# A two-block transformer kernel: table loads by another queue, weight splitting moved around evictions, and the compression's weave re-dealt

## What is computed

```python
h = rms_norm(x, norm_mix)
cols = split_columns(h @ w_in)
o_a = nsa_mixer(cols, ...)      # compressed, selected and window attention
o_b = swa_mixer(cols, ...)      # window attention with sinks
o_c = fox_mixer(cols, ...)      # causal attention with forget gates
proj = jnp.einsum('btnm,nmd->btnd', stack([o_a, o_b, o_c]), w_branch)
gates = jax.nn.sigmoid(cols['merge']).reshape(b, t, 3, 1024)
x = x + (gates * proj).sum(axis=2) @ w_out
x = x + conv_ffn(rms_norm(x, norm_ffn), w_gate, w_up, conv_w, conv_b, w_down)
```

## Time and profile before

| what | value |
|---|---|
| times of the runs | 1562.22, 1564.59, 1554.29 us; median 1562.22 |
| the profiled execution | 1554.0 us |
| its span | 1552.2 us |
| its mean granted TensorE clock | 0.988 |
| PE busy | 1460.3 us, 94% |
| PEld busy | 1196.3 us, 77% |
| DVE busy | 993.6 us, 64% |
| ACT busy | 754.2 us, 49% |
| POOL busy | 67.6 us, 4% |
| DMA | 202.84 MB, mean 131 GB/s |

### The profile page before, as it was taken

How to read it: one execution, slowest core, us unless ns; L and a number is a source line. 1 busy time by engine, 2 the same in 40 slices (tenths; PEclk the granted TensorE clock), 3 DMA queues, 4 the chain that set the end, 5 groups by cost and what they waited for, 6 DMA issues and landing times.

```text
span 1552.2 us, 24143 instructions
## 1 busy us (share of the span) xinstructions
PE 1460.3 (94%) x9392; PEld 1196.3 (77%) x9392; DVE 993.6 (64%) x2286; ACT 754.2 (49%) x1630; POOL 67.6 (4%) x76
## 2 busy tenths in 40 slices
PE   6999999999999999999988999997999899999999
PEld 4777766777778777888766777676787798799987
DVE  3647677564667548545585668766777576777763
ACT  4436566453655443241224546655566347555542
POOL 0000000110000000020000100001101020000000
PEclk9999999999999999999999999999999999999999
DMA  9131180222470322221371144434435542445554
GB/s 364 57 109 55 52 319 25 102 82 68 163 258 1 103 94 82 95 82 55 130 264 54 55 151 110 164 87 139 159 127 157 200 163 93 156 155 187 187 188 136
DMA packets 59866, 202.84 MB, mean 131 GB/s; under 512 B 7694, under 2 KB 10984, under 8 KB 59624
## 3 DMA queue, kind: packets, MB, share of 16 engines
q1 hardware_dynamic: 53568, 192.84, 35.8%
q10 hardware_dynamic: 6008, 7.40, 2.1%
q0 software_dynamic: 176, 1.06, 0.2%
HBM read 199.43 MB, written 1.84 MB: 130 GB/s over the span
## 4 chain that ended last, share of the span: by engine, by line
PE 70%; DVE 15%; DMA 5%; ACT 4%; issue 3%; POOL 2%; SPq 0%; ACTq 0%; DVEq 0%; POOLq 0%
PE ps L2253 65%; PE ps L2256 5%; DVE w_l L2923 3%; DMA w_raw<-in_l_out 1%; DVE st L3022 1%; ACT w_h L2566 1%; DVE x L2931 1%; DVE l_P L2927 1%; DMA w_l_ada<-in_l_ada 1%; DVE m_P L3506 1%; DVE l_xn L2927 1%; DVE l_h_lat L2931 1%; POOL mstat L3600 1%; ACT l_P L2569 1%; DMA w_raw<-in_l_z 1%
## 5 line engine op out<-in xcount | busy, mean ns | idle before, releaser
L2923 DVE TENSOR_TENSOR w_l<-w_raw,w_h 128x1024 fp32r<-128x1024 f32 (+3 forms) x263 | 315.5, 1206 | 76.2 <-ACT w_h L2566 75.4
L2566 ACT ACTIVATE w_h<-w_raw 128x1024 fp32r<-128x1024 f32 (+3 forms) x263 | 272.3, 1042 | 109.5 <-DMA w_raw<-in_f_down 24.1
L2253 PE MATMUL ps<-w_h,l_hTh 128*128 128x512 f32 (+1 forms) x384 | 156.2, 407 | 0.2 <-DVE w_l L2923 0.2
L2253 PE MATMUL ps<-w_h,l_hTl 128*128 128x512 f32 (+1 forms) x384 | 152.0, 396 | 0.0
L2253 PE MATMUL ps<-w_l,l_hTh 128*128 128x512 f32 (+1 forms) x384 | 151.9, 396 | 0.0
L2569 ACT ACTIVATE l_P<-ps,st 128x512 f32<-128x512 f32 (+1 forms) x128 | 77.5, 607 | 88.7 <-DVE st L2931 61.0
L2253 PE MATMUL ps<-f_hTh,w_h 128*128 128x256 f32 x352 | 99.2, 282 | 0.0
L2253 PE MATMUL ps<-f_hTl,w_h 128*128 128x256 f32 x352 | 99.0, 281 | 0.0
L2253 PE MATMUL ps<-l_hTh,w_h 128*128 128x512 f32 (+1 forms) x264 | 98.5, 373 | 0.5 <-issue 0.5
L2253 PE MATMUL ps<-f_hTh,w_l 128*128 128x256 f32 x352 | 98.9, 281 | 0.0
L2253 PE MATMUL ps<-l_hTl,w_h 128*128 128x512 f32 (+1 forms) x264 | 97.8, 370 | 0.0
(11 more groups left out here) (444 smaller groups left out, 3446.5 us busy)
## 6 DMA issues: line engine op xcount, KB each, us to landing
w_raw<-in_l_ada SPq DMA_DIRECT2D x49, 512.0 KB, 5.1
w_raw<-in_l_z SPq DMA_DIRECT2D x32, 512.0 KB, 3.5
w_raw<-in_l_adg SPq DMA_DIRECT2D x32, 512.0 KB, 4.0
w_raw<-in_l_out SPq DMA_DIRECT2D x32, 512.0 KB, 4.5
w_raw<-in_m_merge SPq DMA_DIRECT2D x24, 512.0 KB, 3.3
w_raw<-in_f_gate SPq DMA_DIRECT2D x22, 512.0 KB, 3.2
w_raw<-in_f_up SPq DMA_DIRECT2D x22, 512.0 KB, 3.2
w_raw<-in_f_down SPq DMA_DIRECT2D x22, 512.0 KB, 3.3
```

What stands on the lines that cost most here:

```text
L2253: return p.e.matmul(out, lhsT, rhs, start=start, stop=stop)
L2566: return p.e.activation(out, a, func, scale=scale)
L2923: return p.e.tensor_tensor(out, a, b, op)
```

## The change

Four things are edited.

1. `mix_tables` moves, word for word, from ScalarE's class to GpSimd's (behind `norm_total`), so the six DMAs are issued by GpSimd's queue at the same place of the program.
2. `dense_tok` gets a parameter `late`; with late = 1, which the second half in `last_out` now passes, the split behind the last q of the last group is not emitted. What it would have rounded or split is done by the next `next`.
3. `Weights.rest_all` emits the rests of all blocks that are rounded already; `proj_bkv`'s evac() calls it first.
4. In `second_mix` the compression's weave is written as two, at 8/10 over the first 8 steps and at 16/10 over the others, and attention a's weave is dealt out 14 to 20 with at most 14 steps of gates a, whose last two run after it.

```diff
--- before.py
+++ after.py
@@ -493,7 +493,7 @@
     ff_pad = ff_in = ff_conv = ff_gelu = ff_gated = ff_high = ff_low = idle
 
 
-    def dense_tok(p, name, first, nk, ks, cols, hT, groups, evac):
+    def dense_tok(p, name, first, nk, ks, cols, hT, groups, evac, late=0):
 
         nq = nk // ks
         held = []
@@ -519,7 +519,7 @@
                         evac(t, b, key)
                     if t != group[-1]:
                         yield False
-                if final and not only and q:
+                if final and not only and 0 < q < nq - late:
                     p.W.split_to(held[0].j + NR - 2 + q, held[0].j + NR - 3 + q)
                 yield q == nq - 1
 
@@ -858,7 +858,7 @@
             p.end_with(post, rows, half)
             mix.bias("b", mix.b_free)
         drain(half)
-        half = p.dense_tok(name, 4, 8, 2, 512, x, singles(LAT), evac(1))
+        half = p.dense_tok(name, 4, 8, 2, 512, x, singles(LAT), evac(1), 1)
         tiles(half, 1)
         p.W.split_to(len(p.W.order) + 1, len(p.W.order) + 1)
         rows.norm((0,))
@@ -911,10 +911,14 @@
         m.bias("a", f)
         weave(m.attend("b", f, 4), chain(m.proj_akv(f), m.proj_q("a", f, [LAT]), m.proj_cmp(f), m.branch("c", f)), 28, 13)
         m.flush()
-        weave(m.compress(f, (2, 3)), chain(m.gates("b"), m.branch("b", f)), 24, 20)
+        small, side = m.compress(f, (2, 3)), chain(m.gates("b"), m.branch("b", f))
+        weave(upto(small, 8), side, 8, 10)
+        weave(small, side, 16, 10)
         m.flush()
         f = p.fence()
-        weave(m.attend("a", f, 4), m.gates("a"), 16, 21)
+        side = m.gates("a")
+        weave(m.attend("a", f, 4), upto(side, 14), 14, 20)
+        drain(side)
         p.dense = DENSE
         f = p.fence()
         drain(m.branch("a", f))
@@ -1021,6 +1025,9 @@
             if self.done < len(order) and not order[self.done].is_raw:
                 self.p.w_rest(order[self.done])
             self.done += 1
+
+    def rest_all(self):
+        self.split_to(self.rounded - 1, self.rounded - 1)
 
     def split_more(self, count=1):
         self.split_to(self.rounded + count - 1, self.done + count - 1)
@@ -2000,6 +2007,7 @@
 
         def evac(t, b, tok):
             ps = p.n.bank(b, 288)
+            p.W.rest_all()
             p.mix_gz(self, t, ps, tok, fence)
             p.mix_v(("mix", "v", "b", t), self.bv[:, t, :], ps[:, 128:256], tok, fence)
             x, a, kn, done, todo = self.normed(("m", "bk", t), ps[:, 0:128], 2, tok, fence, self.gain[:, 1])
@@ -2882,18 +2890,6 @@
-    def mix_tables(p, m, fence):
...
@@ -3626,6 +3622,18 @@
     def norm_total(p, m, key, x, nh, a, qs_free, tmp, fence):
         p.power(m.small[:, 64 + 16 * x + 8:64 + 16 * x + 8 + nh], ("norm", "rstd", *key), ("norm", "mean", *key))
 
+    def mix_tables(p, m, fence):
+        n, o = p.n, CONST_AT["hm"][0]
+        p.wait_ge(fence)
+        p.e.dma_start(m.gb[:].rearrange("p a d -> p (a d)"), n.dram["qk_gain_2"].rearrange("l a d -> l (a d)").to_broadcast(
+            [128, 384])).then_inc(*p.landed("d_gb"))
+        p.e.dma_start(m.small[:, 0:8], n.dram["sinks_2"].to_broadcast([128, 8])).then_inc(*p.landed("d_sinks"))
+        p.e.dma_start(m.small[:, 16:57], n.dram["cst"][:, o:o + 41]).then_inc(*p.landed("d_hm"))
+        p.e.dma_start(m.tab[0:32, :], n.dram["rel_bias_2"]).then_inc(*p.landed("d_tab"))
+        for k, name in (("a", "oh_nsa"), ("b", "oh_swa")):
+            o = CONST_AT[name][0]
+            p.e.dma_start(m.oh[k][:], n.dram["cst"][0:33, o:o + 384]).then_inc(*p.landed("d_oh", k))
+
     def fg_neg(p, m, fence):
         p.wait_ge(("forget", "nc"))
         p.e.dma_start(m.fscr, m.f[0][:]).then_inc(*p.landed("d_c"))
```

## The result

The changed kernel takes 1564.88 us (median of 15 runs, 1560.63 to 1566.39); the kernel before, run beside it 15 times, 1556.32 (1551.31 to 1564.59). The ratio is 1.0057, with a 95% interval of 1.0043 to 1.0072: 8.9 us slower (0.0057 × 1556.3), 6.7 to 11.2 by the interval. That is a real loss and less than 1%. Forecast were 1564 us and a loss of 5.

A forecast was written before the change was run, and what follows sets the result against it. TensorE's matmuls, seven tenths of the span, were taken as the bound, so edits count by TensorE's idle and clock. Terms −4.8 −0.9 −0.8 +9.5 +4.5 −0.6 −1.9 = +5.0 on 1559 gave 1564 us; 80% range 1550 to 1579.

The forecast's parts named there:

- part 4: Compression: first weave drains the whole side, 13 chain steps run bare; 58.2 against 48.6 us, +9.5, clock extra.
- The clock's term: Lower TensorE clock after the bare chain's idle, in the logits and attention a: +4.5, between 0 and +7.5.
- Rival C: Clock stays 1.2 GHz from the chain's first long idle into attention a, chain +12, tables only −1.7: +15.4, 1574; chance 0.16.
- part 1: Tables' DMAs on GpSimd's queue: TensorE's stall before the rows' turn (−1.74) and the clock drop behind (−3.1) go: −4.8.
- rival D: Tables arrive late because VectorE's work holds up GpSimd's issuing; all 4.8 lost again: +9.8, 1569; chance 0.08.
- part 2: Round left out behind the second half: −0.9 at l3_out, where TensorE idled 3.10, and 0 at m_out.
- part 3: Weights' rests ahead of bkv's evictions: TensorE's idle of 2.75 before the second block goes, a new short wait follows: −0.8.
- part 5: Attention a and gates a: −0.6 for a wait on GpSimd's addition, −1.9 for two gates steps filling idle before m_aq.
- Rival B: The weave works as its numbers read, 6 + 15 side steps spread over the chain: −9.6, 1549; chance 0.1.
- the base of 1559: Starting time for the forecast, chosen between the profiled execution's 1554.0 and the median of 1562.2.

The follow-up runs named there:

- e1: The kernel before with only the compression's weave split in two as in the change: 1570.7 us, ratio 1.0108 to the kernel before.
- e2: The changed kernel with the first compression weave's side bounded by upto(side, 6): 1550.79 us, ratio 0.9972 to the kernel before.
- e4: The changed kernel with 70 extra unread matmuls (8, 16, 18, 28) in the bare chain's four idle places: 1561.56 us, ratio 1.0046 to the kernel before.
- e9: The changed kernel with the compression woven as before and without rest_all ahead of bkv's evictions: 1549.76 us, ratio 0.9964 to the kernel before.
- e7: The kernel before with only the late split, at l3_out and m_out: 1552.45 us, ratio 0.9985.
- e8: The kernel before with only attention a dealt out 14 to 20 and two steps of gates a behind it: 1553.97 us, ratio 0.9988.
- e6: The kernel before with only the rests ahead of bkv's evictions: 1558.91 us, ratio 1.0014.
- e5: The kernel before with only mix_tables moved to GpSimd's queue: 1553.73 us, ratio 0.9992.

## Why the prediction was right, and where it was not

**The direction and the drain (part 4) were right.** e1 and e2 show it from both sides: +16.8 alone, −13.3 when the side is bounded. e3, the changed kernel with the old weave, undoes this part alone: 8.9 + 5.3 = 14.2. Forecast for it were +9.5 for the bare chain (its own terms, 58.2 less 48.6, give 9.6), +4.5 for the clock and −0.6 in attention a: 13.4.

In the pieces of the trace the stretch grew by 14.6. Hid and side steps took 43.35 us (1218.31 to 1261.66) for the 41.7 of the forecast. The idle there was 0.61 + 1.97 = 2.58, where 1.85 was put, and the clock fell once behind it, which cost 1.7 (0.04 of 43.35). The chain took 19.81 for 16.5, and 6.99 − 3.7 = 3.3 of that is the logits at half speed, so the sum of the chain's rows held. Without the clock's 1.7 and 3.3 the stretch grew by 9.6, as forecast.

**The clock's term was too small.** Attention a's part of it is the 2.4 that e4 saved. 1.7 + 3.3 + 2.4 = 7.4 for the 4.5, the upper end of what was stated. The forecast looked for a drop in the logits and in attention a, and not in the hid phase. That part 4 still came out within a microsecond is partly luck. Draining gives back more in attention a than the 0.6 that was put: from the turn to the last values e4, at full clock, takes 40.58, and e9 takes 42.52, so 2.0. Two idles of 0.59 and 0.81 at the start of e9's attention a are not there.

Rival C was nearer than its chance says. The clock was 0.50 or near it from 1267 to 1286, and behind the chain's first idle it cost 5.7 of C's 9.3. The tables' timed gain of 1.2 is about C's 1.7. What kept C from being the outcome is that the bare chain cost 9.6 and not 12, and what attention a gave back.

**The tables (part 1) did what was said where they stand, and were over-priced.** The stall of 1.74 and the drop behind it are absent in every trace with the edit, and no table came late (in the trace of after m_ohb was in before 910, and its reader ran at 912.62), so rival D falls. From the norm of layer 4 (877.8 before) to 954.5 the eight traces with the edit gain 5.7 to 6.4 us on the trace before, mean 6.1. But of those without it e1 gains 3.3, e7 and e8 1.5 and e6 nothing; with before itself their mean is 1.3, so the edit is worth 4.8 there. Then seven of the eight lose 1.3 to 1.6 again to a drop near 950 (e5's window). At 992 the difference is 4.8 − 1.3 = 3.5, and the timed gain is 1.2 (a loss of 1.7 to a gain of 4.0). The term that failed is the 3.1 for the clock: it was taken from one execution, as if what follows could not draw a drop of its own. Why the new drop comes near 950 no run shows.

**The late split (part 2) was right at both places.** The idle fell from 3.10 to 2.15 (−0.95 for −0.9). At m_out 0 was said; e7 has the same 4.03.

**The rests (part 3) gained nothing of their 0.8.** e6 has +2.2 (−0.6 to +5.1), and e3 and e9, with and without them, are equal, so a small loss isn't shown either. In the trace of after the second block's start was indeed at once, and the third waited 1.45. What was missed in the forecast is that the whole of ck and cv is tied to the chain of VectorE and ScalarE from bkv's evictions, whose end TensorE awaits twice (0.61 and 2.08, unchanged). Of 3 us gained 0.5 were left at the turn at 1096.18. And where the idle of 2.75 had drawn a clock drop, the idles that replaced it drew one behind the 2.08, 3.4 in lost clock instead of 1.7. From 1068.9 to 1221.4 of the trace before, the five traces with the rests lose 1.4 on average on it, the eight without (before among them) 1.1: an edit worth nothing. Why the drop came in some of the traces of either kind and not in others stays open.

**Attention a (part 5)** is −1.6 in e8's trace for the −1.9, and −1.9 timed. The 0.6 for GpSimd's addition was there, since the addition is long done after the change: attention a in the trace of after has no such idle. The 0.79 that e8 shows came in with the new dealing, and the drain takes that away too.

**The sum.** The terms beside part 4 were −9.0, of which 0.6 need the drain. e3 measures 5.3 for the rest, in place of 8.4. So the change lost 8.9 instead of 5: 0.8 of the 3.9 missed lie in part 4 and 3.1 in the other parts, above all the tables' clock and the rests. The predicted 1564 still met the measured 1564.9 by luck, for two errors that offset: the base of 1559 was 2.7 above the median that 15 runs gave (1556.3), and the loss 3.9 too small.

**Rival B**, the weave as its numbers read, is what e2 built. It came out at 1550.8, where the rival gave 1549. That is a gain of 4.4 (2.0 to 6.7), not 9.6.

## What to carry to other kernels

A weave that drains its partner at the end is harmless once and costly when a second weave was to get the rest: bound both sides, and count the steps that are left for the chain. Before you price a wait, ask what the same engine waits for next: what is gained ahead of a longer chain is lost again where its end is awaited (the 2.08 stayed as it was). Matmuls that fill a wait must fit it at half clock too (the 28 of e4 ran 1.6 over). And price what the clock gives back from several executions, not one.

## What the runs showed that had not been expected

**Drops of the clock come and go between executions of the same code.** TensorE's wait of 1.73 to 1.75 before the rows' turn is in the traces of before, e1, e6, e7 and e8. In the first and e6, e7 and e8 the clock fell behind it; in e1 it didn't (window of e1 and of e6, over the same eight us):

```profile
914.00:922.00 8.00, 8.00 (x72) 8.00 (x72) 6.30 (x13) 3.90 (x6) 0.00 (x0) 1.00 0.49 143
```

```profile
914.00:922.00 8.00, 7.18 (x29) 5.05 (x30) 6.98 (x12) 3.18 (x4) 0.00 (x0) 0.64 0.53 188
```

Likewise the idle of 1.0 at 884 was followed by a drop in before, e1 and e6, and by none in the ten other traces. The time lost by one such drop was 1.7 or 3.4 us in the windows of before (1 minus the clock, times the window's length, summed over the drop). The runs of before reach from 1549 to 1565 us, and differences of this kind are as large as what most of the single edits are worth.

**Full TensorE queues don't keep the clock up by themselves** (e4): it fell to 0.50 in matmuls of 16 columns without an idle among them, 2.4 us after the last wait, one of 0.32. By the Trainium skill ("TensorE: Matmul & The Clock Gate", "Part 1: The HAM clock gate (the "warmup" mystery)") the clock goes by how busy the engine has recently been; the trace shows that what the profile counts as busy is not enough for it.

**GpSimd's queue was hardly slower for these loads.** m_gains, m_small twice and m_tab landed after 3.7, 3.7, 3.3 and 3.0 by it, and after 3.2, 3.6, 3.3 and 3.0 by ScalarE's, so by at most 0.5; issuing took 0.52 to 0.77 instead of 0.34 to 0.46.
